# Decoding attention with exponentials under block maxima, the state step among the last heads, and a reordered preparation, in a one-core layer kernel

## The reference, cut to what matters

```python
kmean = jnp.mean(kb, axis=3)                       # kb: blocks of 256 tokens = 2 pages
gate = einsum('bhqd,bhnd->bhqn', q, kmean)
_, sel = lax.top_k(gate, 3)                        # 3 of the 4 past blocks, and the own block
s = einsum(q, k[selected]) * hd ** -0.5
p = softmax(s)
o = einsum(p, v[selected])
# delta rule, decoding: S = exp(g) S + k (beta (v - k.(exp(g) S)));  o = q . S
```

## Time and profile before

| | us |
|---|---|
| median of three runs | 591.93 (591.51 to 597.29) |
| the profiled execution | 592.36 |
| its span in the trace | 590.6 |

### The profile page before, as it was taken

One profiled execution on the slowest core, in us unless ns is written; L12 is line 12 of the kernel. 1 busy time (PEld: TensorE's weight loads), 2 busy tenths in 40 slices (PEclk: granted clock), 3 DMA queues, 4 the chain that ended last, 5 costly groups with the idle time before them and its releaser, 6 DMA issues.

```text
span 590.6 us, 10244 instructions
## 1 busy us (share of the span) xinstructions
PE 536.5 (91%) x3943; PEld 450.6 (76%) x3943; DVE 350.1 (59%) x550; ACT 164.4 (28%) x233; POOL 55.7 (9%) x125
## 2 busy tenths in 40 slices
PE   7889999897997889888699689888999999999997
PEld 6567767674796767666464169688999999999996
DVE  4441578576987979854753556555664665555441
ACT  4102114512033212221001133462434343423420
POOL 6800000000107500000101000000000000000000
PEclk8879998996799999999888799997999999999999
DMA  9996574294087658462569997684556564545201
GB/s 292 339 306 199 175 248 156 73 246 162 19 273 246 220 175 283 148 205 84 180 215 378 369 321 234 213 267 144 166 192 191 166 198 146 192 155 185 74 18 38
DMA packets 98919, 116.53 MB, mean 197 GB/s; under 512 B 6301, under 2 KB 81262, under 8 KB 98854
## 3 DMA queue, kind: packets, MB, share of 16 engines
q1 hardware_dynamic: 93218, 104.42, 55.3%
q10 hardware_dynamic: 3908, 7.42, 3.5%
q0 software_dynamic: 1744, 4.04, 2.6%
HBM read 113.04 MB, written 2.99 MB: 196 GB/s over the span
## 4 chain that ended last, share of the span: by engine, by line
PE 68%; DVE 19%; DMA 6%; ACT 3%; issue 2%; ACTq 1%; DVEq 0%
PE bank L336 64%; DVE prod L943 4%; DVE s_all L1063 4%; DVE mats L943 3%; DMA ring<-in_ada_w_dram 2%; DMA ring<-in_w_out_dram 2%; DVE BTP L943 1%; DVE cv L1171 1%; DMA ring<-in_cache_v_dram 1%; DMA x_nat<-in_x_sample_dram 1%; PE bank L373 1%; ACT w_part L1752 1%; PE bank L382 1%; PE bank L544 1%; DVE w_ab L943 0%
## 5 line engine op out<-in xcount | busy, mean ns | idle before, releaser
L336 PE MATMUL bank<-a_hi,w_part 128*128 128x264 f32 x832 | 154.4, 287 | 2.1 <-DVE a_lo L1508 2.1
L943 DVE TENSOR_TENSOR w_part<-ring,w_part 128x2048 fp32r<-128x2048 f32 (+1 forms) x38 | 84.9, 2236 | 90.2 <-ACT w_part L1752 90.2
L336 PEld LDWEIGHTS bank<-a_hi,w_part 128*128 128x128 f32 x832 | 130.6, 191 | 2.6 <-issue 2.6
L336 PE MATMUL bank<-a_lo,w_part 128*128 128x264 f32 x416 | 118.9, 286 | 0.0
L1752 ACT ACTIVATE w_part<-ring 128x2048 fp32r<-128x2048 f32 (+1 forms) x38 | 70.9, 1871 | 86.9 <-PE bank L336 75.0
L336 PE MATMUL bank<-hT,ring 128*128 128x264 f32 x352 | 84.3, 398 | 1.8 <-ACT proj L1599 1.8
L336 PEld LDWEIGHTS bank<-hT,ring 128*128 128x128 f32 x352 | 67.7, 195 | 16.1 <-issue 4.5
L336 PEld LDWEIGHTS bank<-a_lo,w_part 128*128 128x128 f32 x416 | 79.5, 191 | 0.1
L336 PE MATMUL bank<-hid_hi,w_part 128*128 128x264 f32 x352 | 64.9, 285 | 0.0
L336 PEld LDWEIGHTS bank<-hid_hi,w_part 128*128 128x128 f32 x352 | 54.5, 188 | 0.1
L336 PEld LDWEIGHTS bank<-ident 128*128 128x128 f32 x344 | 47.3, 219 | 9.3 <-issue 5.6
(11 more groups left out here) (333 smaller groups left out, 576.4 us busy)
## 6 DMA issues: line engine op xcount, KB each, us to landing
ring<-in_ada_w_dram SPq DMA_DIRECT2D x24, 1024.0 KB, 7.1
ring<-in_cache_k_dram SPq DMA_DIRECT2D x64, 256.0 KB, 3.7
ring<-in_w_in_dram SPq DMA_DIRECT2D x11, 1024.0 KB, 5.4
ring<-in_w_gate_dram SPq DMA_DIRECT2D x11, 1024.0 KB, 5.3
ring<-in_w_up_dram SPq DMA_DIRECT2D x11, 1024.0 KB, 5.3
ring<-in_cache_v_dram SPq DMA_DIRECT2D x40, 256.0 KB, 4.3
ring<-in_w_down_dram SPq DMA_DIRECT2D x8, 1024.0 KB, 5.1
ring<-in_cache_v_dram ACTq DMA_DIRECT2D x24, 256.0 KB, 5.2
```

The lines of the kernel that those rows point to most:

```text
L336: return pe.matmul(out, lhsT, rhs, start=start, stop=stop, skip_group_check=True)
L943: return v.tensor_tensor(out, a, b_, op)
```

## The change

The diff has four parts.

1. **Weights under block maxima.** The samples are taken in two groups of four. For each group G sums and transposes the scores and DVE forms maxima over tokens; DMAX spreads them and subtracts each block's own maximum from its scores; ACT writes the exponentials straight into the columns that the V products read. V0 needs `p_ready` 1, from group 0 alone; the ranking of the blocks (RK), the denominators (DEN) and the final weights come beside the V stages. The value products of a group accumulate in one bank, a block in 32 rows each (a half of V now holds one page of each of the four blocks). After V3 and V7 ACT copies the bank out, WC turns the weights, and FO folds them in with 16 small products.
2. **The states earlier.** XA, XB and XC stand in and behind H6 and H7, in banks 3, 6 and 7; the fillers of H6 and H7 go from 18 and 6 to 10 and 4. K15 and the heads are followed by A8; A9 stands behind V6 in `ORDER` and in the ring.
3. **The preparation.** GN, DNORM, GC, KSUM, KB, GBC, ROWS, KK follow each other with no W or K between them; the projections and K stages that stood there come behind KK. The betas' part of GN becomes KB.
4. **Issue of the pages.** SP issues all pages; ACT issues none. The fillers before the decoding attention's products (8, 9, 5, 9, 8, 4) go; FO has 6.

```diff
-    ORDER = ("W1 W2 QS W7 K0 CEXT W8 K1 QSUM W9 K2 QNORM W10 CONV BA AB W3 DSUM K3 W4 DNORM KSUM K4 GN W5 "
-             "K5 GC KNORM GBC KR ROWS KK W6 K6 TI VR L1 K7 KROW W0 K8 M1 VROW L2 K9 M2 TAILS L3 S K10 M3 A4 "
+    ORDER = ("W1 W2 QS W7 K0 CEXT W8 K1 QSUM W9 K2 QNORM W10 CONV BA AB W3 DSUM W4 K3 GN DNORM GC KSUM KB GBC ROWS "
+             "KK K4 W5 KNORM TI K5 KR L1 W6 K6 M1 VR KROW L2 K7 M2 VROW W0 K8 L3 TAILS S K9 M3 A4 H0 K10 L4 M4 K11 "
...
-            first = q * NPG + hf * PGI
-            pages = [eng.value_load(table[0:1, first + k:first + k + 1], min_val=0, max_val=NPHYS - 1) for k in part]
+            index = [q * NPG + (PPB * k + hf if kind == "v" else hf * PGI + k) for k in part]
+            pages = [eng.value_load(table[0:1, n:n + 1], min_val=0, max_val=NPHYS - 1) for n in index]
...
-                for _ in range((14, 8, 2, 16, 4, 4, 18, 6)[h]):
+                for _ in range((14, 8, 2, 16, 4, 4, 10, 4)[h]):
...
+            def group_sums(g):
+                pe.wait_ge(sem("k_scored"), GS * (g + 1))
+                b = opened(f"gsT{g}", (3, 6)[g])
+                for n in range(2):
+                    o = g * GW + n * P
+                    pe.transpose(b[:, GW + n * P:GW + (n + 1) * P], s_all[:, o:o + P], ident[:, :])
+                closed(mm(b[:, 0:GW], ones[:, :], s_all[:, g * GW:(g + 1) * GW]), f"gsT{g}")
+
+            def spread_max(g):
+                pe.wait_ge(sem("max_diag"), g + 1)
+                b = opened(f"pmax{g}", (3, 5)[g])
+                closed(mm(b[:, 0:GW], ones[:, :], w_a[:, g * GW:(g + 1) * GW]), f"pmax{g}")
...
             def page_values(q):
-                if q == 0:
-                    keep_awake(4, 9)
-                    pe.wait_ge(sem("p_ready"), 1)
-                b = opened(f"pv{q}", 4 + q % 2)
+                g, j = q // GS, q % GS
+                if j == 0:
+                    pe.wait_ge(sem("p_ready"), g + 1)
+                    opened(f"pv{g}", (7, 4)[g])
+                b = bank[(7, 4)[g]]
...
+            def fold():
+                keep_awake(6, 6)
+                pe.wait_ge(sem("selw"), 1)
+                pe.wait_ge(sem("pv_rows"), 2)
+                b = opened("y8", 6)
+                for g in range(2):
+                    for c in range(AC):
+                        for h2 in range(2):
+                            r = 64 * h2
+                            last = mm(b[r:r + 64, c * NS + g * GS:c * NS + (g + 1) * GS],
+                                      pv_out[g][:, c * P + r:c * P + r + 64], selw[:, g, 2 * c + h2, :])
+                closed(last, "y8")
...
+            def spread_max(g):
+                b = full(v, f"pmax{g}")
+                freed(v.tensor_reduce(of(top4, g), b[:, 0:GW].rearrange("p (n t h) -> p n h t", t=PPB, h=H), AX, ALU.max),
+                      f"pmax{g}")
+                v.wait_ge(bank_free[filled[f"pmax{g}"][0]], frees_at(f"pmax{g}"))
+                s = paged(s_all[:, g * GW:(g + 1) * GW])
+                inc(tt(s, s, bc(of(top4, g).unsqueeze(2), [P, GS * NB, PPB, H]), ALU.subtract), "shifted")
...
+            def fold(_):
+                own_v = w_a[:, 256:256 + AC * NS].rearrange("p (c q) -> p c q", c=AC)
+                v.wait_ge(sem("wgt"), 1)
...
+                freed(tt(mixT[:, PCH:PCH + AC, T:NT], b[:, 0:AC * NS].rearrange("p (c q) -> p c q", c=AC), own_v, ALU.add), "y8")
...
+            def page_exps(g):
+                a.wait_ge(sem("shifted"), g + 1)
+                a.wait_ge(sem("p_zeroed"), g + 1)
+                s = s_all[:, g * GW:(g + 1) * GW].rearrange("p (j n h) -> p j n h", n=NPG, h=H)
+                inc(a.activation(p_own[g], s, ACT.Exp, scale=SCALE), "p_ready")
...
-            def value_pages(q):
-
-                if q == 0:
-                    a.wait_ge(sem("table_in"), 16)
-                if q + 2 < NS:
-                    for hf in range(HALVES):
-                        item = ("v", (q + 2, hf))
-                        load_pages(a, item, range(PGI // 2, PGI))
...
-                    load_pages(sp, it, range(PGI // 2 if kind == "v" and i[0] >= 2 else PGI))
+                    load_pages(sp, it, range(PGI))
```

More of the change, by code:

```diff
@@ L580, in dn_heads, with dn_betas @@
                 closed(last, "gn")
+            def dn_betas():
                 for c in range(GC):
@@ L780, in page_values @@
                     slot = arrived(pe, ("v", (q, hf))).rearrange("p (k n) -> p k n", k=PGI)
-                    for k in range(PGI):
-                        last = mm(b[32 * k:32 * k + 32, :], pP[:, q * NPG + hf * PGI + k, :], slot[:, k, :],
-                                  hf == 0, hf == HALVES - 1)
-                    if hf < HALVES - 1:
+                    for k in range(NB):
+                        last = mm(b[32 * k:32 * k + 32, :], pP[g][:, j * NPG + PPB * k + hf, :], slot[:, k, :],
+                                  j + hf == 0, j == GS - 1 and hf == HALVES - 1)
@@ new lines, in denominators, with turn_weights @@
+            def denominators():
+                pe.wait_ge(sem("p_ready"), 2)
+                b = opened("den", 6)
+                for g in range(2):
+                    last = mm(b[:, g * GW:(g + 1) * GW], ones[:, :], p_own[g])
+                closed(last, "den")
+            def turn_weights():
+                pe.wait_ge(sem("wgt"), 1)
+                b = opened("wcol", 5)
+                for g in range(2):
+                    last = mm(b[:, g:g + 1], w_a[:, g * P:(g + 1) * P], ident[:, 0:1])
+                closed(last, "wcol")
@@ L1209, in dn_heads, with dn_betas @@
                 v.sem_inc(sem("gn_out"), 1)
+                for n in range(TT):
+                    last = tt(P1[:, n, :, :], bc(triu[:, :].unsqueeze(1), [P, GH, P]),
+                              bc(gn[:, n, 1, :].unsqueeze(2), [P, GH, P]), ALU.mult)
+                inc(last, "ug")
+            def dn_betas(_):
                 for c in range(GC):
@@ L1404, in denominators @@
[L1404 to L1419 removed]
+                v.wait_ge(sem("w_exp"), 1)
@@ new lines, in block_weights, with turn_weights @@
+                inc(last, "wgt")
+            def turn_weights(_):
+                b = full(v, "wcol")
+                every = [P, 2, H * GS]
+                freed(tt(selw[:, :, :, :].rearrange("p g h j -> p g (h j)"),
+                         bc(selq[:, :, :].rearrange("p h j -> p (h j)").unsqueeze(1), every),
+                         bc(b[:, 0:2].unsqueeze(2), every), ALU.mult), "wcol")
+                v.wait_ge(bank_free[5], frees_at("wcol"))
+                v.sem_inc(sem("selw"), 1)
@@ new lines, in fold @@
+            def fold(_):
+                own_v = w_a[:, 256:256 + AC * NS].rearrange("p (c q) -> p c q", c=AC)
+                v.wait_ge(sem("wgt"), 1)
+                for h2 in range(2):
+                    r = slice(64 * h2, 64 * h2 + 64)
+                    last = tt(own_v[r, :, :], proj[r, VC0:VC0 + AC, T:NT],
+                              sm64[r, 5, :, :].rearrange("p q (c w) -> p w c q", w=2)[:, h2, :, :], ALU.mult)
+                step(last)
+                b = full(v, "y8")
+                freed(tt(mixT[:, PCH:PCH + AC, T:NT], b[:, 0:AC * NS].rearrange("p (c q) -> p c q", c=AC), own_v, ALU.add), "y8")
+                v.wait_ge(bank_free[6], frees_at("y8"))
+                v.sem_inc(sem("mix"), 1)
@@ L1852, in _ @@
             step(g.memset(blk[:, :], 0.0))
-            step(g.memset(selc[:, :, :], 0.0))
-            step(g.memset(dm8[:, :], 0.0))
+            step(g.memset(selq[:, :, :], 0.0))
+            for n in range(NB):
+                step(g.memset(bidx[:, n, :], float(n + 1)))
             step(g.memset(i64[:, :], 0.0))
```

239 lines of the change are left out of this document (95 added, 144 removed).

## The result

The changed kernel is slower: 615.96 us (614.88 to 620.32) against 593.09 us for the kernel before in the same session, a ratio of 1.0388 (95% interval 1.0311 to 1.0465). The prediction had the sign and 5 us; it is 22.9 us. The profiled executions are 615.08 and 592.36 us, with spans of 613.4 and 590.6.

The account below looks back on a forecast made before the run. Bound by the chain of waits up to the output projection's first matmul at 350.56, nearly all products after. -0.5 + 13.0 + 0.8 - 6.1 - 5.3 + 3.3 = +5.2 on 592.36: forecast 597, 8-in-10 range 584 to 604.

Parts of the forecast that it names:

- the front: From 119.3 to 213.7, stages reordered with no operation removed: 0.5 us earlier, bounds 5 us gained to 4 lost.
- `wout`'s landing: From `wout`'s issue to its landing: 5.3 us without a backlog instead of 11.41, so -6.1, bounds 0 and -6.1.
- the clock: Half-clock stretches: +2.3 us for XB's spread, UD and A8, +1.0 for V7, FO and fillers; together +3.3, bounds 0 and +9.
- second rival: In the front: the preparation keeps its gain and loses none at W0, -4 instead of -0.5, 594 us; chance 0.13.
- A7 to A8: G0, DMAX0, OWN, XA and XB put between them delay A8's first item by 13.0 us, bounds 4.7 and 18.
- first rival: Between A7 and A8: the heads take the states in, A8 is read only 6 us later, 588 us; chance 0.17.
- fourth rival: Clock stays low through A8 and again into the output projection: +9 instead of +3.3, 603 us; chance 0.15.
- SP's issue: V stages, SP issuing all pages at 4.34 us per item: `wout` goes 55.1 us after the first, +0.8.
- third rival: V stages: issue is hidden, pages stream at the DMAs' pace, with clock and front 584 us; chance 0.10.
- Landing to first matmul: From `wout`'s landing to the output projection's first matmul: 4.6 us instead of 10.0, -5.3; -2.5 if FO comes last.

Follow-up runs that it names:

- d_front: Block maxima alone (old front order, state places and ACT issue) plus the new order of the front and of K9 to K11: 597.72 us, 1.0061 of the kernel before.
- a_awake: Changed kernel with fillers 24 and 8 ahead of heads 6 and 7, 8 ahead of the own tokens' spread and 8 ahead of XB's: 610.14 us, ratio 1.0269.
- c_best1: Block maxima alone, with RK behind XC, A9 in front of V0, and 18 and 6 fillers ahead of heads 6 and 7: 588.38 us, ratio 0.9891.
- a_states: Changed kernel with XA, XB, XC beside V1 to V3 again and G0, DMAX0, OWN behind A8: 606.85 us, ratio 1.0218.
- a_act: Changed kernel with ACT again issuing two of the four pages of each half from V2 on: 603.94 us, ratio 1.0174.
- d_sp: Block maxima alone (old front order, state places and ACT issue) but all pages issued by SP: 596.6 us, 1.0086 of the kernel before.
- c_best2: c_best1 with G0 and DMAX0 between A7 and UB, V0 behind A9, and OWN, G1, DMAX1 beside V0 to V2: 585.35 us, ratio 0.9863.

## Why the prediction was wrong

The place was right. Nothing moved behind the output projection's first matmul, and four of five pieces had the right sign. The sum was short by 17.6 us: 8.2 in the front, 4.0 between A7 and A8, 3.4 on SP, 3.1 at `wout`'s landing, less 1.1 behind it.

**The front is the step that failed, in mechanism and not only in size.** "TensorE is the late one ... about 34 us of it from 151.7, and S can start VectorE at 186.3." S's mask came at 193.00. The preparation did end 9.2 us earlier on TensorE (W5 begins at 145.09, the like projection before at 154.26), near what I had placed. But from there to S's scores TensorE now has three projections and 46.9 us, where it had two and 36.2: the third had run inside the preparation while VectorE did K4. I had counted all three, and their work was nearly right. What I put at nothing were the waits and the clock. W5 took 9.25 us instead of 7.3 and ended at 154.3, not 151.7. From there it took 37.6 us to S's product, with 3.3 us of waits for VectorE's copy and the tails. VectorE's part of the preparation ended at 150.1, not near 144.5, so its gain of 2 to 3 us was not there either.

How much S moved is open: in the five kernels with the changed kernel's code up to there the mask came at 190.6 to 193.0, in six with the order of before at 191.4 to 197.4. What is firm is that the 5 us did not come, and what follows. From the mask to A7 it takes 63.4 to 63.5 us in all seven kernels with the old order and 69.5 to 70.9 in all seven with the new. Of that K9 is 4.7, which I had. The rest I had at nothing: with K9, K10 and K11 ahead of H1's probabilities TensorE waits for them and then runs at the lower clock. In the changed kernel, W5, H1's turn and A5:

```profile
145.09 9.25 PE L345 MATMUL bank<-hT,ring 128*128 128x264 f32 x32
...
220.89 0.90 PE L553 MATMUL bank<-ident,smpT 128*128 128x128 f32 x3 [6.32 <-DVE smpT L1095]
...
223.19 2.30 PE L345 MATMUL bank<-ring,cT 128*32 128x256 f32 x32
```

A5 takes 2.30 to 3.64 us in the seven kernels with the new order and 1.93 in all others. Together this is the +7.7: S 1.6, K9 4.7, the rest 1.4. d_front shows 1.2% for the whole part. My second rival, a gain kept, was wrong in the same step.

**A7 to A8** was the right mechanism. The row of steps gave 13.0, and with the clock 15.3; it is 19.3. a_awake puts at least 3.2 us on the clock (I had 2.3), so the steps are 16 at most. Among them are VectorE's two operations of head 6 at 0.88 and 0.81 us (below) and the fillers that went: with 10 and 4 instead of 18 and 6, A8 follows A7 after 21.1 to 22.4 us in the four kernels with the old places, at a granted clock of 0.77 to 0.84, and after 19.0 in c_best1, at 1.00. The first rival, in which the heads take the states in, is refuted: 16.7 us between a_states and the changed kernel. The fourth, a clock low through A8 and into the output projection, did not come either: it was 0.50 from 281 to 291, but A8 took 1.93 us and the 12 fillers 2.94, both at full clock.

**SP's issue.** The step of 4.34 us was right (4.29 measured), the third rival wrong. The 3.4 us missed are two: V0 had not been read when SP stood at V2's second half (its turn at 310.3, issued at 312.51), and the last two halves were issued 5.4 us apart behind A9's items (353.10, 358.50), with the four issues taking 3.00 us at a DMA share over 1. I had checked the first of them with V0 8.4 us behind A8; it was 10.1, and V0's 16 products took 3.07 us. The 240 GB/s of the page traffic were called under what the rows show; the rows named reach 238, but the trace has 373 from 305 to 345. The Trainium skill ("DMA: Bandwidth & Descriptors", Issuing engines are not separate DMA queues) says that issue on several engines saves only the sequencer's time, usually small beside the DMA. It is not small here: a second issuing engine is worth 12 us (a_act) and 9 us (d_sp), since four reads and four issues of 256 KB pages take 4.3 us, and the halves come 2.9 us apart once ACT helps.

What the forecast did not see at all is how a price of SP's issue can hide in a comparison. Before, ACT's help and the late V0 cancelled: 54.3 us from half to `wout`, of which SP's queue stood still for V0 from about 287.6 to 301.5. I compared 55.1 with 54.3 and called it 0.8. The change freed V0 from the whole softmax and then could not use it, since its own late A8 and SP's pace took its place. The block maxima alone are worth 3.6 us, and with places that suit them and the old fillers (c_best2) 8.

**`wout`'s landing** was mis-sized: 8.4 us, not 5.3. I took the backlog as gone; but A9's second item (10.4 us to land) and V7 go out directly ahead, and the DMA share is 1.07 from 350 on. Landing to first matmul was right (4.8 against 4.6).

**The range** ended at 604, though the upper bounds of the terms add up to much more: 4 + 18 + 0.8 + 0 - 2.5 + 9 = 29.3, which is 621 (a low clock between A7 and A8 is in two of them). It left room for one term to miss, the fourth rival's 603, and four missed the same way. Two came out beyond what was allowed them: the front (+7.7, bound +4) and SP's term (+4.2, which had no bound).

## What to carry to other kernels

Work that is taken out of a stretch must be entered where it goes: before calling a preparation shorter, add up each engine's work from its new end to the next meeting point, with its waits for the other engine and the clock after them (here 34 us of work took 37.6, and the projection ahead of it 9.25 instead of 7.3). A chain that alternates between two in-order engines is not absorbed by their idle time; put it beside transfers that run anyway. Before moving DMA issues to one queue, divide its time per item (reads of the address and issues, here 4.3 us) by the time of the transfer (here 2.9); above one, the queue is the pace, even if the kernel before hides it behind another wait.

## What was not expected of the hardware

Two kernels with the same code up to there differ by 3 us in one projection: after the same wait of 3.4 us on TensorE, the granted clock was 1.00 or 0.55 (W4 above, 7.36 or 10.40 us). Of the five profiled executions with this wait W4 was slow in four; in the seven where it was 2.0 us or less W4 took 7.36 each time, and with a 2.9 us row of fillers in the wait too.

XA's and XC's 64 products with one moving column took 3.27 us at full clock and 5.78 at a granted clock of 0.50; the times in between (4.58, 3.90) have a change of the clock in them. In the kernel before, XC ran at full clock and the products of V3 right behind it took 2.50 us instead of 1.92, granted 0.78. Whether such products let the clock fall is not shown.

VectorE slows down beside a GpSimd memset. In the changed kernel, head 6's first scaling, then the memset that ran beside it, and the same operation of head 5 without one:

```profile
273.47 0.88 DVE L1094 TENSOR_SCALAR smpT<-smpT,st 128x128 f32<-128x128 f32 x1
```

```profile
273.30 0.97 POOL L1999 MEMSET prod<- 128x1056 f32 x1 [52.34 <-DVE s_all L1073]
```

```profile
257.67 0.29 DVE L1094 TENSOR_SCALAR smpT<-smpT,st 128x128 f32<-128x128 f32 x1
```

That is 0.5 us on the path to A8. The same operation takes 0.88 us in all thirteen kernels with this memset, which starts 0.2 us ahead of it each time, and 0.29 in the kernel before, which has none there. The Trainium skill ("GPSIMD Engine Reference", 1. Specifications) names an SBUF interface that GpSimd shares with VectorE, with contention for VectorE's instructions in a two-port mode or with two SBUF inputs. The rows agree with contention; no run here shows the mode of the instruction.
